# Four-layer hybrid transformer in fp32: full attention taken two steps at a time, and the starts of three attention loops rearranged

## The reference, cut to what matters

```python
# layer A: 8 query heads of 64 on 2 key/value heads, full attention, beside a two-way state-space mixer
h = rms_norm(x, norm_mix_w[i]); proj = h @ w_in[i]
q, k, v, z, xbc_raw, dt_raw = split(proj)
q, k = axial_rope(rms_norm(q)), axial_rope(rms_norm(k))
s = einsum("bqgrd,bkgd->bgrqk", q / 8, k); p = softmax(s); attn_out = einsum("bgrqk,bkgd->bqgrd", p, v)
ssd_out = ssd_mixer(z, xbc_raw, dt_raw, ...)      # depthwise conv of 5 taps, chunked scan, gated norm
x = x + concat([attn_out, ssd_out]) @ w_out[i]
x = x + (silu(rms_norm(x) @ w_gate) * (rms_norm(x) @ w_up)) @ w_down
# layer B: windowed attention of 8 heads with a sink, beside differential attention of 4 heads
ya = windowed_gqa_sink(qa, ka, va, sink)          # blocks of 128, one block to either side
w = softmax(q1 k1) - lam * softmax(q2 k2); yb = rmsnorm(w @ v) * (1 - lambda_init)
x = x + concat([ya, yb]) @ w_out[l];  x = x + (silu(conv3(gate)) * val) @ w_down
```

## Time and profile before

| | us |
|---|---|
| median of 3 runs | 2441.34 (2438.64 to 2444.68) |
| the profiled execution | 2441.04 |
| its span, first to last instruction | 2439.3 |
| PE busy | 2389.9 (98%) |
| DVE busy | 1427.6 (59%) |
| ACT busy | 934.6 (38%) |
| POOL busy | 274.7 (11%) |

### The profile page before, as it was taken

How to read it: one execution, slowest core, us unless ns; L and a number is a source line. 1 busy time by engine, 2 the same in 40 slices (tenths; PEclk the granted TensorE clock), 3 DMA queues, 4 the chain that set the end, 5 groups by cost and what they waited for, 6 DMA issues and landing times.

```text
span 2439.3 us, 30895 instructions
## 1 busy us (share of the span) xinstructions
PE 2389.9 (98%) x12492; PEld 1970.8 (81%) x12492; DVE 1427.6 (59%) x1950; ACT 934.6 (38%) x1468; POOL 274.7 (11%) x199
## 2 busy tenths in 40 slices
PE   8999999999999999999999999999999999999999
PEld 7777888888877788888887778888888777888887
DVE  6876444445587644343567766555466776645554
ACT  5574322223446532222444752222234475322222
POOL 2013100001200300000232410000012212000000
PEclk9999999999999999999999999999999999999999
DMA  5110222223211122222221112222232111222222
GB/s 188 69 36 28 94 104 88 102 90 118 88 70 36 35 89 101 104 89 101 104 88 69 36 35 94 96 104 93 97 108 99 53 36 53 87 104 87 104 91 99
DMA packets 31101, 205.32 MB, mean 84 GB/s; under 512 B 3440, under 2 KB 3568, under 8 KB 7408
## 3 DMA queue, kind: packets, MB, share of 16 engines
q1 hardware_dynamic: 30960, 203.35, 23.4%
HBM read 201.24 MB, written 2.10 MB: 83 GB/s over the span
## 4 chain that ended last, share of the span: by engine, by line
PE 89%; DVE 7%; ACT 1%; issue 1%; DVEq 1%; ACTq 0%; POOL 0%; DMA 0%; SPq 0%
PE bank L1656 26%; PE bank L1658 26%; PE bank L1657 26%; PE bank L1778 2%; PE bank L1839 2%; PE bank L1815 2%; DVE a_conv L1077 1%; DVE neg_max L1450 1%; PE bank L1761 1%; DVE b_p L1462 1%; PE bank L1826 1%; PE bank L2061 0%; PE bank L2259 0%; PE bank L2078 0%; PE bank L2235 0%
## 5 line engine op out<-in xcount | busy, mean ns | idle before, releaser
L818 DVE TENSOR_TENSOR w_lo<-w_raw,w_hi 128x2048 fp32r<-128x2048 f32 (+1 forms) x180 | 411.2, 2284 | 392.3 <-ACT w_hi L341 391.8
L1656 PE MATMUL bank<-h_ffn_hi,w_hi 128*128 128x512 f32 x1408 | 548.6, 390 | 0.0
L1658 PE MATMUL bank<-h_ffn_hi,w_lo 128*128 128x512 f32 x1408 | 547.8, 389 | 0.0
L1657 PE MATMUL bank<-h_ffn_lo,w_hi 128*128 128x512 f32 x1408 | 547.7, 389 | 0.0
L341 ACT ACTIVATE w_hi<-w_raw 128x2048 fp32r<-128x2048 f32 (+1 forms) x180 | 340.9, 1894 | 462.6 <-PE bank L1658 433.8
L1658 PEld LDWEIGHTS bank<-h_ffn_hi,w_lo 128*128 128x128 f32 x1408 | 264.3, 188 | 55.3
L1657 PEld LDWEIGHTS bank<-h_ffn_lo,w_hi 128*128 128x128 f32 x1408 | 264.3, 188 | 54.7
L1656 PEld LDWEIGHTS bank<-h_ffn_hi,w_hi 128*128 128x128 f32 x1408 | 264.3, 188 | 54.4
L1656 PE MATMUL bank<-act_hi,w_hi 128*128 128x512 f32 x704 | 273.9, 389 | 0.0
L1657 PE MATMUL bank<-act_lo,w_hi 128*128 128x512 f32 x704 | 273.9, 389 | 0.0
L1658 PE MATMUL bank<-act_hi,w_lo 128*128 128x512 f32 x704 | 273.9, 389 | 0.0
(11 more groups left out here) (325 smaller groups left out, 3413.5 us busy)
## 6 DMA issues: line engine op xcount, KB each, us to landing
w_raw<-weights SPq DMA_DIRECT2D x184, 1024.0 KB, 4.8
w_raw<-weights SPq DMA_DIRECT2D x4, 544.0 KB, 3.8
w_raw<-weights SPq DMA_DIRECT2D x8, 256.0 KB, 6.2
residual<-x_in SPq DMA_DIRECT2D x8, 256.0 KB, 6.2
x_out<-residual SPq DMA_DIRECT2D x8, 256.0 KB, 2.0
cst<-consts SPq DMA_DIRECT2D x1, 966.0 KB, 9.3
par_b<-params_b SPq DMA_DIRECT2D x1, 627.0 KB, 10.2
par_a<-params_a SPq DMA_DIRECT2D x1, 244.0 KB, 2.6
```

What stands on the lines that cost most here:

```text
L818: nc.vector.tensor_tensor(w_lo[s][:, cols], w_raw[s][:, cols], w_hi[s][:, cols].bitcast(F32), ALU.subtract).then_inc(w_ready, 1)
L1656: mm(out, ahi, bhi, start=start, stop=False)
L1657: mm(out, ahi, blo, start=False, stop=False)
L1658: return mm(out, alo, bhi, start=False, stop=stop)
```

## The change

Five things are changed.

1. **Full attention, two steps at a time** (A layers). The order of PE for i = 4, 6, ... 18 is now: S(i), S(i + 1), T(i - 2), F if i is a multiple of 4, V(i - 4), V(i - 3), T(i - 1). S(0) and S(1) are both issued inside the z projection, T(0) comes before S(2), and the turn of the last query tile goes between T(0) and S(2), through other banks (`TURN_A`).
2. **ACT and DVE in these loops**: C(i - 2) for odd i now comes behind both exponentials of ACT; DVE takes M(i) and M(i + 1) together from i = 4.
3. **Rotation of the last tile** (A layers): its products are moved behind the fifth convolution block and `conv_start(6)`, its sum and scaling behind `conv_start(7)`.
4. **Output rows**: of the eight `out_rows`, the last two are moved behind the last `y_products`.
5. **B layers**: T(0) of the windowed attention is issued at step 1 instead of step 2, with the second eviction of `b_vb` moved behind E(0) on ACT; D(0) is issued ahead of the windowed T(15) and D(1) behind V(15), with the reduction and exponentials of D(0) taken in the windowed loop.

```diff
 # ACT, A layers
-                for i in range(20):
-                    if i == 1:
-                        for m in (4, 5):
-                            turned_hi(m)
+                pair_exp(lay, 0, 0, 512, probs)
+                pair_exp(lay, 0, 1, 512, probs)
+                pair_exp(lay, 1, 0, 512, probs)
+                pair_exp(lay, 1, 1, 512, probs)
+                turned_hi(4)
+                pair_copy(lay, 0, 512, pts)
+                turned_hi(5)
+                for i in range(2, 20):
                     if 4 <= i < 12:
                         split_quarter(lay, g0 + 9 + i // 4, i % 4)
                     if i < 16:
                         pair_exp(lay, i, 0, 512, probs)
-                    if 2 <= i < 18:
+                    if 3 <= i < 18 and i % 2 == 0:
                         pair_copy(lay, i - 2, 512, pts)
                     if i < 16:
                         pair_exp(lay, i, 1, 512, probs)
+                    if 3 <= i < 18 and i % 2 == 1:
+                        pair_copy(lay, i - 2, 512, pts)
...
 # ACT, B layers
-                for half in range(2):
-                    evict_pair(g0 + 7, half, lambda t: B["b_vb"][:, t, :])
+                evict_pair(g0 + 7, 0, lambda t: B["b_vb"][:, t, :])
...
+                for par_ in range(2):
+                    pair_exp(lay, 0, par_, window(0)[1] * P + 1, probs)
+                evict_pair(g0 + 7, 1, lambda t: B["b_vb"][:, t, :])
+                pair_copy(lay, 0, window(0)[1] * P, pts)
+                for i in range(1, 20):
...
+                    if i == 18:
+                        diff_exp(0, 0)
+                        diff_exp(0, 1)
...
 # DVE, A layers
                 conv_start(5)
-                rope_a(3)
                 conv_taps(4)
                 conv_start(6)
+                last_tile = products_a(3)
                 conv_taps(5)
                 conv_start(7)
+                finish_a(3, last_tile)
                 split_lo(g0 + 9)
...
+                pair_max(lay, 1)
                 take_gate()
...
-                    if i < 16:
+                    if i < 4:
                         pair_max(lay, i)
+                    if 4 <= i < 16 and i % 2 == 0:
+                        pair_max(lay, i)
+                        pair_max(lay, i + 1)
...
 # DVE, B layers
                 window_max(0)
+                pair_copy(lay, 0, window(0)[1] * P, pts)
...
+                    if i == 17:
+                        diff_max(0)
...
-                for i in range(20):
+                for i in range(1, 20):
                     if i < 16:
                         diff_max(i)
-                    if i == 0:
+                    if i <= 16:
+                        diff_coef(i - 1)
+                    if i == 1:
                         out_lo(lay, 3, B["b_on"], B["b_ot_hi"], B["b_ot_lo"])
-                    if 1 <= i <= 16:
-                        diff_coef(i - 1)
...
 # PE
+            def full_attention(lay, q_of, k_of, v_of, probs, pts, before_turn, before_scores, inside):
+                for i in range(1, 4):
+                    if i in before_scores:
+                        before_scores[i]()
+                    if i >= 2:
+                        pair_scores(lay, i, False, q_of, k_of, False)
+                    if i < 3:
+                        before_turn[i]()
+                        pair_turns(lay, False, i - 1, probs)
+                for i in range(4, 20, 2):
+                    for n in (i, i + 1):
+                        if n < 16:
+                            pair_scores(lay, n, False, q_of, k_of, False)
+                    if i < 18:
+                        pair_turns(lay, False, i - 2, probs)
+                    if i % 4 == 0:
+                        pair_factors(lay, i // 4 - 1)
+                    pair_values(lay, False, i - 4, v_of, pts)
+                    if i in inside:
+                        inside[i]()
+                    pair_values(lay, False, i - 3, v_of, pts)
+                    if i < 18:
+                        pair_turns(lay, False, i - 1, probs)
...
                 def first_scores():
                     pe.wait_ge(t_free, base + 4)
                     pair_scores(lay, 0, False, query_rows, key_rows, False)
+                    open_bank(0, g0 + 10)
+                    open_bank(1, g0 + 10)
+                    pair_scores(lay, 1, False, query_rows, key_rows, False)
...
-                    if w >= 6:
+                    if w == 6:
                         pe.wait_ge(sm_ready, 4 * lay + 4)
-                        out_rows(1, 2 * w - 12)
-                        out_rows(1, 2 * w - 11)
+                        out_rows(1, 0)
+                        out_rows(1, 1)
                     y_products(w)
+                for k in range(2, 4):
+                    out_rows(1, k)
...
-                                13: lambda: turned(7), 17: lambda: turned(8)},
+                                13: lambda: turned(7), 17: first_diff},
...
+                                7: turn_first_key, 10: turn_second_key, 11: lambda: turn_diff(6), 14: turn_last_key, 18: lambda: diff_scores(1)},
+                               [1] + list(range(3, 18)))
...
-TURN_A = (5, 6, 7, 4, 7, 4, 5, 6, 5, 6)
+TURN_A = (5, 6, 7, 4, 4, 3, 5, 6, 5, 6)
```

More of the change, by code:

```diff
@@ L1829, in pair_attention @@
-                    if i >= 3:
-                        u = i - 3
-                        t, j = divmod(u, 4)
-                        k0, nb = blocks(u)
-                        if j == 0 and t >= 1:
-                            pe.wait_ge(o_free, 4 * lay + t)
-                        for par_ in range(2):
-                            pe.wait_ge(ptc[par_], 16 * lay + u + 1)
-                        for b in range(nb):
-                            for par_ in range(2):
-                                last = mm(bank[4][par_ * HD:(par_ + 1) * HD, j * P:(j + 1) * P], v_of(j // 2, k0 + b),
-                                          pts[u % 2][par_][:, b * P:(b + 1) * P], start=(b == 0), stop=(b == nb - 1))
-                                if b == nb - 1:
-                                    last.then_inc(o_done, 1)
+                    if 2 <= i < 16:
+                        pair_scores(lay, i, True, q_of, k_of, True)
@@ L2214, in turned, with diff_scores @@
                     pe.wait_ge(t_free, base + 6 + n)
-                pair_attention(lay, True, query_rows, key_rows,
-                               lambda g, b: B["b_va"][:, b, g * HD:(g + 1) * HD], True,
+                def diff_scores(i):
+                    t, h = divmod(i, 4)
+                    if i >= 2:
+                        pe.wait_ge(de_done, 32 * l + 2 * (i - 2) + 2)
+                    ts_ = slice(t * P, (t + 1) * P)
+                    for n, (qt, kt) in enumerate(((h_mix_hi, kt_hi), (h_mix_hi, kt_lo), (h_mix_lo, kt_hi))):
+                        for c in range(2):
+                            rows = slice(c * HD, (c + 1) * HD)
+                            last = mm(bank[DS_BANKS[i % 2][c]][:, :], qt[rows, 4 + h, ts_], kt[rows, h, :],
+                                      start=(n == 0), stop=(n == 2))
+                            if n == 2:
+                                last.then_inc(ds_done, 1)
@@ new lines, in diff_turns, with diff_values @@
+                def diff_turns(u):
+                    pe.wait_ge(dw_done, 16 * l + u + 1)
+                    if u >= 2:
+                        pe.wait_ge(dptc, 16 * l + u - 1)
+                    for b in range(TB):
+                        last = nc.tensor.transpose(bank[(7, 0)[u % 2]][:, b * P:(b + 1) * P],
+                                                   probs[u % 2][0][:, b * P:(b + 1) * P], ident)
+                    last.then_inc(dpt_done, 1)
+                def diff_values(u):
+                    t, h = divmod(u, 4)
+                    pe.wait_ge(dptc, 16 * l + u + 1)
+                    if u == 0:
+                        pe.wait_ge(r_taken, 4 * lay + 4)
+                    if u == 4:
+                        pe.wait_ge(o_free, 4 * lay + 4)
+                    if h == 0 and t >= 2:
+                        pe.wait_ge(do_free, 4 * l + t - 1)
+                    for b in range(TB):
+                        last = mm(bank[DO_BANKS[t % 2]][:, h * P:(h + 1) * P], pts[0][u % 2][:, b * P:(b + 1) * P],
+                                  B["b_vb"][:, b, h * P:(h + 1) * P], start=(b == 0), stop=(b == TB - 1))
+                    last.then_inc(do_done, 1)
@@ L2262, in _ @@
+                for i in range(2, 19):
+                    if i < 16:
+                        diff_scores(i)
+                    if i < 18:
+                        diff_turns(i - 2)
+                    if i >= 3:
+                        diff_values(i - 3)
                 w_out(lay, g0 + IN_B, base, 14, B["b_ot_hi"], B["b_ot_lo"], B["b_dm"], mix_ready, l + 1, (do_free, 4 * l + 3), False)
```

204 lines of the change are left out of this document (100 added, 104 removed).

## The result

| | kernel before | kernel after |
|---|---|---|
| median, us (9 runs each) | 2441.32 (2438.64 to 2444.68) | 2449.70 (2446.81 to 2450.48) |
| ratio to before | | 1.0033, 95% interval 1.0025 to 1.0041 |
| the profiled execution, us | 2441.04 | 2446.81 |
| its span, us | 2439.3 | 2445.0 |
| full attention, first score to the mixer's first state product, first / second layer | 58.2 / 58.0 | 62.2 / 61.9 |

A forecast was written before the change was run, and what follows sets the result against it. PE, busy 98% of the span, was taken as the bound. Attention +2.0, rotation -1.4 and rows -0.25 in two A layers gave +0.7, B layers -1.3: -0.6 against 2441.04, so 2440.5 us, range 2431.5 to 2447.5.

The forecast's parts named there:

- Fewer changes between kinds of matmuls: Full attention loop: fewer entries into scores, value products and whole-array work save 2.3 us for each A layer.
- rival 1: Full attention loop: PE stays the bound, each A layer gains 2.2 us instead of losing 2.0, total 2432.1; chance 0.25.
- The circle through ACT: Full attention loop: a 6.33 us chain of waits pauses PE about 0.75 before S(7), S(9), S(11), S(13), 3.0 us.
- a weight quarter (0.56): Full attention loop: the 0.56 us counted for a weight quarter on ACT within the 6.33 us circle.
- I take 0.1 for S(15): Full attention loop: without a quarter the circle is 5.77 us, about PE's own 5.55, leaving 0.1 us before S(15).
- T(14): End of the full attention: T(14) waits for C(13), 3.2 us after V(10), a pause of 1.4 us.
- The beginning: Start of the full attention: pauses of 0.5, 0.8 and 0.8 us at T(0), S(4) and S(5), together 2.1.
- +2.0 for each A layer: Full attention, net: 2.0 us longer in each A layer, bounds -2.2 and +3.
- Rotation: A layers, last tile: PE's 1.34 us pause goes, -1.4 us for each A layer, bounds -1.6 and 0.
- Output rows: A layers, behind `y_products(7)`: 0.25 of PE's 1.72 us pause goes, -0.25 for each A layer, bounds -1.4 and 0.
- B layers: D(0), D(1) early: -0.5 us each B layer; T(0) early: at most 0.3 gained in the last layer, 0 in the third.
- rival 2: Full attention: the clock falls to half, up to 3.4 us each; three falls give 2450.7; chance 0.10.

The follow-up runs named there:

- three_probs: Kernel after with a third pair of buffers for the probabilities alone: 2446.67 us, ratio 1.0025 to the kernel before.
- rest_only: Kernel after with the full attention in its old order: 2441.32 us, ratio 0.9999 to the kernel before.
- no_drain: Kernel after with the drain behind the fourth weight quarter moved from i = 7, 11 to i = 8, 12: 2447.33 us, ratio 1.0024 to before.
- copies_behind: Kernel after with both weight quarters of a turn ahead of E(i) and C(i - 2) behind both exponentials of step i: 2448.29 us, ratio 1.0028.
- b_only: Kernel before with the whole B layers' change alone: 2444.08 us, ratio 1.0009; the second time 2442.61 us, ratio 1.0002.
- rotation_only: Kernel before with the last tile's rotation split alone: 2437.63 us, ratio 0.9984.
- three_buffers2: Kernel after with third pairs of buffers for both the probabilities and their transposes: 2437.39 us, ratio 0.9986 to the kernel before.
- best_no_b: Three pairs of buffers of both kinds, rotation split and output rows moved, B layers as in the kernel before: 2433.64 us, ratio 0.9973.
- early_turn_only: Kernel before with only T(0) of the windowed attention early in the B layers: 2439.13 us, ratio 1.0000; run again 2440.62 us, ratio 0.9998.

## Why the prediction was wrong

It said 2440.5, with 2431.5 to 2447.5 for the range; it is 2449.7, a case (over 2448.7) to which it gave a chance of 0.13, mostly for a fall of the clock in the full attention that didn't come. The order of events in the attention was forecast rightly and most pauses came where it put them. The sizes were short. Of the profiled executions, +5.8 us was measured where -0.6 was forecast. The 6.4 between them are 3.8 in the two attentions (points 2 to 4), 0.5 for the output rows (point 6) and 2.0 in the B layers (point 7). The median run adds 2.9 more, with its lower clock.

1. **Fewer changes between kinds of matmuls, 2.3 us for each A layer: right.** With both chains cut two steps take 5.53 us (5.55 forecast), and the attention is 2.0 and 1.8 us shorter than before, although listed pauses of 2.1 us are left in it, as many as before. That is rival 1's case, priced there at 2.2; it needed two more pairs of buffers.
2. **The circle through ACT: right, with a term mis-sized.** Before S(7) and S(11), 0.74 was lost where 0.75 was forecast. The step that failed is "a weight quarter (0.56)": its row shows a quarter without a drain. Behind every fourth stands one, in the middle of the circle: 0.57 more was lost before S(9) and 0.28 more before S(13), 0.85 in all. Without it those two pauses fell from 1.04 and 0.74 to 0.55 and 0.47. The drain by itself is 0.28 of each (last section; in three_probs they are 0.76 and 0.74). The other 0.3 before S(9) came from the drain and the second chain of point 3 together, and nearly all of it went when either was taken out.
3. **"I take 0.1 for S(15)": wrong, because a second chain was missed.** E(i + 1) overwrites what T(i - 1) reads. In the old order T(i - 1) was a step away; in the new one it stands at the end of the turn, behind both value products, and only S(i + 2) is between it and S(i + 3). It costs 0.53 wherever the first chain doesn't cost more. T(14) lost 1.83 instead of 1.4, 0.3 of that for the same reason: in the chain that it waits for, ACT stood 0.3 us ahead of E(15), which started at 169.59, until T(13) was done, and in three_probs, where it needn't, T(14)'s pause is 1.41 instead of 1.72. The text asked of C(i - 2) what it waits for, and not of E(i + 1), though the list ahead of it has that wait ("E(i) waits for M(i) and for T(i - 2)"). That makes 0.7 us, and 0.1 of T(14) stays unexplained.
4. **The beginning: pauses priced as the profile lists them.** A listed pause is what is left once the matmuls before it have run out; the start is late by 0.17 more. For T(0), S(4) and S(5) the text took 0.5, 0.8 and 0.8, by the 0.78 listed in the earlier trace rows; they list 0.41, 0.66 and 0.64, and lost 0.57, 0.83 and 0.80, with 0.1 in each score's group behind it: 0.3 short. Points 2 to 4 together come to 2.0; +2.0 for each A layer fell short of +3.9 by 1.9.
5. **Rotation: right in the second layer, 0.9 in the first.** The split of w_lo "ends at about 107.8, when PE comes to it": it ended at 107.84, but PE could have come at 106.8 (the turn at 106.42 and 0.35 for it), and 0.87 is listed. From the third turn of a convolution block to S(0) 29.45 us are left of 30.32: 0.9 gained. In the second layer 0.47 is listed and 1.4 gained, as forecast, but in part by luck: beside the pause of 1.37 another of 0.27 on `a_bct` went, and the one on w_lo came. All profiles with the split have 29.4 to 29.6 and 28.7 to 29.0 in the two layers there, those without it 30.3 to 30.4 in both. So the split gives 2.3 us in this stretch, not 2.8; of the 1.35 by which S(0) came earlier in the first layer, 0.5 lie ahead of it, in a start that was earlier.
6. **Output rows: nothing instead of -0.25.** PE's pause on L672 fell from 1.72 to 1.17, but PE now waits 0.29 for a mask product ahead of it. All kernels, with the rows moved or not, need 40.8 us for this stretch.
7. **B layers: the steps gave 0.4 us and not 1.3, and the clock took more.** D(0) and D(1) early gave 0.4 in each layer (the fourth's differential part 50.4 to 50.1), where 0.5 was forecast. T(0) early gave 0.4 in the fourth layer (the windowed part 48.3 to 47.9), where 0.3 was forecast. In the third, where the text took 0 and half a clock, it cost: at full clock the windowed part takes 48.7 to 49.0 us in the five profiles without the early turn and 49.5 to 49.8 in the five with it. The term that failed is that 0: M(1) and the turn behind it come late there, as the rows with the pause of 1.80 show. The clock was priced only as a rival, and for another place. In the A layers' attention it stayed full with all those pauses, in this trace and in all others of this study; it fell in the B layers instead. The rule of the Trainium skill ("TensorE: Matmul & The Clock Gate", Part 4: PE-mode transpose), that transposes don't count as activity in the same way, spoke for rival 2; no run here shows it at work in that loop.

How much that is can be read from the runs' mean clocks. Of the kernels with both moves in the B layers (after, rest_only, no_drain, copies_behind, the three with more buffers, b_only both times) 7 of 93 runs had a mean clock of 0.999 or 1.000; of the kernel before it was 54 of 134, of the kernels with one of the moves 26 of 52, of those with neither but other parts 23 of 37. At 0.999 the kernel before takes 2438.2 to 2441.8 us (the middle one 2439.2), at 0.997 2442.2 to 2443.8 (2443.1). So the steps' small gain in the B layers is taken back and more: rest_only against rotation_only is +3.7 us, three_buffers2 against best_no_b +3.8, b_only against before +2.9 and +1.0 (the interval of the first touches no difference, that of the second holds it). That both moves together go with the lower clock is shown by the counts; why together and not each alone isn't, and stays open. How far these 1.0 to 3.8 us are the clock's and how far the early turn's in the third layer isn't separated either. Also open is why the early turn has runs at 0.995 to 0.997 beside runs at 1.000.

By medians the loss divides into +8.4 for the attention (after against rest_only), -3.6 for the rotation and +3.7 for the B layers with the rows (rest_only against rotation_only). These add up by how they are formed, and confirm nothing.

## What to carry to other kernels

When an order is packed tighter, list for every instruction that moves closer all the buffers that it writes, and who reads them last: here two chains were nearly of one length, and cutting either alone gave less than a third. Third buffers, laid into memory that was unused at that time, turned a loss of 3.9 us for each attention into a gain of 1.9. A step that is brought forward also pushes back what it now stands ahead of on each queue, as T(0)'s copy did with M(1). Price pauses by starts, from a group to where the next would have started, and look at what the queue itself holds, drains too.

## What the runs showed of the hardware

- A drain in ACT's queue cost the overlap with the next instruction. In three_probs, from a weight quarter to the exponential behind it takes 0.52 us, and 0.80 with a drain between them, whose buffers and maxima were ready both times:

```profile
135.76 0.63 ACT L360 ACTIVATE w_hi<-w_raw 128x512 fp32r<-128x512 f32 x1
136.28 0.69 ACT L450 ACTIVATE a_p<-bank,neg_max 128x512 f32<-128x512 f32 x1
...
142.08 0.63 ACT L360 ACTIVATE w_hi<-w_raw 128x512 fp32r<-128x512 f32 x1
142.88 0.69 ACT L450 ACTIVATE a_p<-bank,neg_max 128x512 f32<-128x512 f32 x1 [0.17 <-PE bank L1849]
```

- The falls of the clock to half lasted 3.4 or 6.8 us in all profiles but for two stretches at the very end of a span, and came at different places in executions of the same kernel (b_only: three stretches, near 1333, 1384 and 1992 us; again: near 1384, 1940 and 1988). PE had pauses just ahead of each: here are the stretches before the two falls of after, where it was busy for 1.60 and 1.64 of 3.4 us. Such pauses alone don't decide, as the third row shows, from the kernel before: PE busy for 0.96 of 3.4 us, and the clock full there and behind it.

```profile
1336.40:1339.80 3.40, 1.60 (x22) 1.24 (x18) 1.68 (x4) 2.84 (x10) 0.00 (x0) 1.00 0.00 0
1387.60:1391.00 3.40, 1.64 (x11) 0.99 (x12) 3.25 (x7) 1.90 (x6) 0.00 (x0) 1.00 0.00 0
...
1380.00:1383.40 3.40, 0.96 (x6) 0.49 (x6) 3.23 (x6) 2.46 (x7) 0.00 (x0) 1.00 0.00 0
```

- Runs of one kernel on one chip fall into groups by their clock: early_turn_only has six runs at 1.000 with 2438.3 to 2439.1 us, one at 0.999 with 2440.8 and four at 0.996 or 0.997 with 2443.0 to 2444.4. A difference of under 3 us in this kernel is told only by many runs, with their clocks beside them.
- The full clock held in the A layers' attention of all 19 profiles read here, with up to nine pauses between 0.3 and 1.7 us in it and a third of its time transposes.
